# A two-layer encoder on eight cores: pooling sums as one VectorE scan, no tensor work on GpSimd, norms as concurrent tasks

## The chip, the cores and the metric

The kernel runs on all 8 cores of one Trainium2 chip (two dies of four cores). Every core runs the same program on its own tokens; there is no communication between cores. The metric is the device time in microseconds of the slowest core.

## The reference

`x_prompt` is (2, 8192, 1024) and `x_sample` (16, 2048, 1024), both float32. Two layers with their own weights are applied to both. One layer is:

```python
h = rmsnorm(x, g_pre_mix)
u = h @ w_in                      # 1024 -> 6144: pool | B | C | V | gate a | gate b
# pooling: channel group i of 256 has window w = (2, 4, 8, 16)[i]
d = mean(g[t - w/2 .. t + w/2 - 1], valid positions only) - g[t]
y_a = concat(d @ pool_w[i]) * pool_scale
y_b = B * dwconv3_centred(C * V)  # depthwise, over positions
m = sigmoid(ga) * y_a + sigmoid(gb) * y_b
x = x + rmsnorm(m @ w_out, g_post_mix)
f = rmsnorm(x, g_pre_ffn)
hid = silu(f @ w_ffn_gate) * (f @ w_ffn_up)      # 1024 -> 2816
x = x + rmsnorm(hid @ w_ffn_down, g_post_ffn)
```

## The kernel before

Data lie with channels on the 128 partitions and tokens along the free axis. A core has three segments of 2048 tokens (two sample rows, a quarter of a prompt row with a halo), cut into two tiles each: `NT` = 6 tiles a layer and 12 tiles n = 0..11 in all. A tile is some 1032 tokens wide, worked on as two halves i = 0, 1 of w columns. Where the halves of a tile's mixing stage are wider than 512 columns (516 to 528; all tiles but n = 1, 3, 7, 9), `pieces` cuts each half in two, so that a matmul there has 258 to 264 columns and not 512.

The stages of a tile:

- `stage_M` (mixing): 8 channel blocks of 128, three weight units each (`sect` 0 to 2). A unit is a `quad`: a Strassen-Winograd scheme over the two halves with 7 products (P1, P5, P2, P6, P3, P7, P4) of 4 matmuls. It reads seven combinations of h in `h_t`, made beforehand by `combos`, and seven of the weights. Each product is taken out of its PSUM bank by ScalarE (activation, copy to `ss`) or VectorE (`tt` with `ss`, `tm` or `z_t`). `take` and `give` hand out five banks for products and two for copies. Per block, behind the products: `conv` (ScalarE, then two VectorE taps of 1024 columns), `windows` (pooling sums, log2(w) doubling additions of some 1030 columns on GpSimd), and `join` (s1 to s4, four VectorE instructions of 1024 columns).
- `stage_OP`: the output projection, 128 matmuls of 512 columns at most; ScalarE copies to `o_t` and squares for the norm (`Tree`, VectorE adds the squares pairwise).
- `stage_GU`: gate and up as 22 quads; ScalarE does the SiLU, the product with the second half's `up` is made on GpSimd (L982), the first half's on VectorE.
- `stage_D`: down projection, 352 matmuls, also to `o_t`.

The program order of a round n is M(n), 4 units of GU(n-1), OP(n), the other 18 units of GU(n-1), D(n-1). Three background generators run between the PE items: `chain_task` (after OP: post-mix norm, residual with the x tile loaded again, store, pre-FFN norm, `combos`), `post_task` (after D: post-FFN norm, accumulated into DRAM by DMAs of the GpSimd queue) and `pre_task` (x loaded, squared, loaded once more and scaled into `h_t`, `combos`). `rstd` inside them sums over partitions with tiny matmuls (L420), takes the power -0.5 on GpSimd (L434), and sends the row through DRAM (`rsc`) and back to all partitions (`rb`).

Order: the generator keeps a virtual time `stt_["vt"]`, which only `adv` moves, by the matmuls' cost at full clock. `pump` issues what is due: one-shot callbacks (`after`) and steps of the background list `bg`. The list is first in, first out: only its head runs. `finish_bg(tag)` runs everything up to the tagged task to its end at once, without moving the virtual time. Each engine works its instructions strictly in this program order, with semaphore waits derived by `Sched`. VectorE's queue thus holds both PSUM evictions, for which PE waits, and background work.

```python
bg.append([stt_["vt"], gen, tag])                      # L267
tt("pool", zf(Z_T1 + lo, Z_T1 + hi), upr(lo - 1, hi - 1), upr(lo, hi), ALU.add)   # L752
while step * 2 < wd: ...                               # L754, doubling on GpSimd
item(clock["slot"], lambda n=n: finish_bg(("post", n - 2)))                        # L1110
stage_GU(n - 1, 0, 4)
stage_OP(n)
item(..., add_bg(pre_task(n + 1, hold=lambda n=n: gu_done.get(n - 1)), ...))       # L1114
stage_GU(n - 1, 4, JC)
item(clock["slot"], lambda n=n: finish_bg(("chain", n)))                           # L1117
stage_D(n - 1)
```

Weights come as float32 in the first tile of a layer (GpSimd-queue DMAs with a cast), get their Winograd sums on VectorE (`prep`, four additions), and are kept in DRAM; later tiles load them prepared. Four slots hold units in the order of use. Before the first tile, `prologue` folds `pool_w` into the pool columns of `w_in`: 8 groups, both layers, 16 matmuls each.

## Time and profile before

| | us |
|---|---|
| times of 3 runs | 6272.72, 6577.19, 6615.12 |
| median | 6577.19 |
| the profiled execution, its own time | 6255.55 |
| its span on the slowest core (core 1) | 6254.0 |
| spans of the 8 cores | 6207.1 to 6254.0 |
| mean granted TensorE clock, all cores | 0.900 to 0.905 |
| busy: PE, VectorE, ScalarE, GpSimd | 5035.1, 3543.9, 2521.5, 1631.8 |

The span is from the first to the last instruction of one core; the time is the device time of the same execution. The profiled execution lies near the lowest of the three times. Busy PE counts matmuls with modelled ends, so a stage is better judged by matmuls per microsecond. The granted clock is a share of 2.4 GHz; 0.5 is 1.2 GHz.

### The profile page before, as it was taken

How to read it: one execution, taken by the hardware profiler on the slowest of the kernel's cores; microseconds unless marked ns; L12 is line 12 of the kernel's file. 1: busy time of each engine (PE TensorE's matmuls, PEld its weight loads, DVE VectorE, ACT ScalarE, POOL GpSimd, SP SyncE). 2: the span in 40 equal slices, each digit the busy share in tenths (PEclk: the TensorE clock that was granted, in tenths of full speed). 3: DMA queues.
4: the chain of work that ended last, by engine and by line, in shares of the span. 5: the costliest groups of instructions: out<-in, count | busy, mean ns of one | idle time of the engine just before them, and what ended most of it. 6: DMA issues, size and time to landing. Idle time of an engine off the chain costs nothing.

```text
span 6254.0 us, 92792 instructions; the slowest of 8 cores (6207.1 to 6254.0 us)
## 1 busy us (share of the span) xinstructions
PE 5035.1 (81%) x29350; PEld 2934.2 (47%) x29350; DVE 3543.9 (57%) x5521; ACT 2521.5 (40%) x5253; POOL 1631.8 (26%) x1644
## 2 busy tenths in 40 slices
PE   2778875887996897789589897679789789968987
PEld 1543334533433653678467543364334365445433
DVE  3768546554654753754776567275385375465521
ACT  0444433442542452454245353245345244434432
POOL 0323213132231230422323223132143032131221
PEclk6899988998997898899899998889999888979998
DMA  7765885365564464545756559555556454553553
GB/s 168 166 169 139 186 200 136 100 197 133 148 191 117 124 177 132 131 145 171 152 156 203 148 157 222 150 135 163 158 150 189 133 131 138 167 130 113 178 142 91
DMA packets 289209, 959.65 MB, mean 153 GB/s; under 512 B 43098, under 2 KB 44250, under 8 KB 288730
## 3 DMA queue, kind: packets, MB, share of 16 engines
q1 hardware_dynamic: 242074, 838.29, 44.4%
q0 software_dynamic: 46656, 115.43, 12.3%
q8 instruction: 246, 4.03, 0.3%
q14 instruction: 233, 1.91, 0.1%
HBM read 813.27 MB, written 205.32 MB: 163 GB/s over the span
## 4 chain that ended last, share of the span: by engine, by line
PE 57%; DMA 16%; DVE 15%; issue 7%; POOL 2%; ACT 1%; SPq 0%; DVEq 0%; POOLq 0%; ACTq 0%
PE bank L339 57%; DVE z_t L317 4%; DMA x_t<-xss 3%; DMA x_t<-xsin 3%; DMA rb<-rsc 3%; DMA rsc<-r 3%; DVE h_t L317 2%; DVE z_t L308 2%; DVE tm L308 2%; DVE h_t L308 2%; DVE o_t L317 2%; DMA x_t<-xps 1%; DVE slot L308 1%; POOL o_t L308 1%; DMA x_t<-xpin 1%
## 5 line engine op out<-in xcount | busy, mean ns | idle before, releaser
L339 PE MATMUL bank<-h_t,slot 128*128 128x258 f16 (+3 forms) x22064 | 3706.1, 331 | 1049.9 <-DVE tm L308 424.6
L339 PEld LDWEIGHTS bank<-h_t,slot 128*128 128x128 f16 x22064 | 2217.9, 102 | 2503.8 <-issue 1317.5
L339 PE MATMUL bank<-z_t,slot 128*128 128x512 bf16 (+1 forms) x6720 | 1298.4, 356 | 16.2 <-DVE z_t L308 15.3
L303 ACT ACTIVATE ss<-bank 128x258 f32<-128x258 f32 (+3 forms) x1576 | 737.9, 468 | 743.8 <-PE bank L339 732.4
L308 DVE TENSOR_TENSOR sq<-sq 128x512 bf16<-128x512 bf16 (+3 forms) x672 | 366.1, 555 | 1084.2 <-ACT sq L303 1078.5
L339 PEld LDWEIGHTS bank<-z_t,slot 128*128 128x128 bf16 x6720 | 665.1, 99 | 636.8 <-issue 108.0
L303 ACT ACTIVATE bank<-bank 128x512 f32<-128x512 f32 (+3 forms) x788 | 360.3, 457 | 1314.9 <-PE bank L339 1296.1
L308 DVE TENSOR_TENSOR tm<-bank,ss 128x512 f32<-128x512 f32 (+3 forms) x936 | 526.4, 564 | 305.8 <-PE bank L339 240.6
L308 POOL TENSOR_TENSOR z_t<-z_t 128x1038 f32<-128x1038 f32 (+6 forms) x240 | 550.6, 2294 | 534.2 <-ACT z_t L303 494.7
L308 POOL TENSOR_TENSOR z_t<-tm 128x512 bf16<-128x512 f32 (+1 forms) x308 | 376.0, 1221 | 902.2 <-DVE tm L308 550.9
L303 ACT ACTIVATE o_t<-bank 128x512 f32<-128x512 f32 (+1 forms) x448 | 239.2, 534 | 706.6 <-PE bank L339 683.4
L434 POOL TENSOR_TENSOR r<-v,half 128x4 f32<-128x4 f32 (+3 forms) x96 | 107.6, 1121 | 1560.4 <-DVE v L430 1553.5
L303 ACT ACTIVATE sq<-o_t 128x512 bf16<-128x512 f32 (+1 forms) x576 | 362.9, 630 | 311.2 <-POOL o_t L308 267.1
L317 DVE SCALAR_TENSOR_TENSOR z_t<-z_t,cs 128x1024 f32<-128x1024 f32 (+1 forms) x192 | 419.9, 2187 | 27.9 <-ACT z_t L303 14.8
L317 DVE SCALAR_TENSOR_TENSOR o_t<-o_t,cs,rb 128x512 f32<-128x512 f32 (+1 forms) x384 | 375.4, 992 | 101.8 <-DMA rb<-rsc 101.8
L308 DVE TENSOR_TENSOR z_t<-bank,ss 128x258 f32<-128x258 f32 (+3 forms) x640 | 304.9, 476 | 218.1 <-ACT ss L303 113.2
L317 DVE SCALAR_TENSOR_TENSOR z_t<-z_t 128x1024 f32<-128x1024 f32 (+1 forms) x288 | 360.4, 1252 | 7.4 <-POOL z_t L308 3.6
L308 POOL TENSOR_TENSOR o_t<-o_t,x_t 128x512 f32<-128x512 f32 (+1 forms) x192 | 256.4, 1340 | 380.0 <-DVE o_t L317 290.6
L308 DVE TENSOR_TENSOR z_t<-bank,tm 128x512 bf16<-128x512 f32 (+1 forms) x308 | 188.2, 611 | 294.2 <-PE bank L339 293.1
L303 ACT ACTIVATE z_t<-bank 128x258 f32<-128x258 f32 (+3 forms) x640 | 273.0, 426 | 69.0 <-PE bank L339 56.9
L317 DVE SCALAR_TENSOR_TENSOR h_t<-x_t,cs,rb 128x516 f16<-128x516 f32 (+3 forms) x192 | 141.3, 754 | 235.3 <-DMA x_t<-xss 95.4
L308 DVE TENSOR_TENSOR z_t<-tm,z_t 128x258 f32<-128x258 f32 (+3 forms) x320 | 221.7, 693 | 34.7 <-DVE tm L308 1.8
(43 smaller groups left out, 2071.8 us busy)
## 6 DMA issues: line engine op xcount, KB each, us to landing
slot<-wqs SPq DMA_DIRECT2D x460, 896.0 KB, 5.9
wqs<-slot SPq DMA_DIRECT2D x92, 896.0 KB, 6.3
slot<-wds SPq DMA_DIRECT2D x80, 704.0 KB, 4.4
x_t<-xsin SPq DMA_DIRECT2D x128, 256.0 KB, 5.3
x_t<-xss SPq DMA_DIRECT2D x128, 256.0 KB, 5.0
slot<-wgu POOLq DMA_DIRECT2D x44, 512.0 KB, 8.8
slot<-wos SPq DMA_DIRECT2D x40, 512.0 KB, 3.5
rb<-rsc SPq DMA_DIRECT2D x68, 256.0 KB, 6.0
```

What stands on the lines that cost most here:

```text
L303: S.op("act", (lambda a, o=out.ap, i=in_.ap, f=func, kw=kw: a.activation(out=o, in_=i, func=f, **kw)), reads=keys(rd), writes=keys([out]))
L308: v.tensor_tensor(out=o, in0=a, in1=b, op=op)), reads=keys([in0, in1]), writes=keys([out]))
L317: v.scalar_tensor_tensor(out=o, in0=a, scalar=s, in1=b, op0=op0, op1=op1)),
L339: ins = pe.matmul(o, lhsT=a, rhs=b, start=(start and i == 0), stop=(stop and i == n - 1), skip_group_check=True)
L434: S.op("pool", (lambda e, o=r.ap, a=v.ap, b=half[0:bs, 0:nb]: e.tensor_tensor(out=o, in0=a, in1=b, op=ALU.pow)), reads=keys([v]) + [("half ...
```

## The change

- `windows`: for w = 4, 8, 16 the sums over the window are one `tensor_tensor_scan` on VectorE (running sum: add the entering token, subtract the leaving one), and its last value before the tile's end is kept in `hist` for the next tile. For w = 2 it is one subtraction, which replaces s1 as well. The edge correction moves to VectorE.
- The residual addition of the chain and the second half's hidden product go from GpSimd to VectorE. GpSimd keeps small copies and memsets, the power in `rstd`, and its DMAs.
- The two conv taps are issued as two callbacks at different times; the scan is issued after section 2's P7; s1 to s4 are spaced wider.
- `pump` picks the due background task of lowest time, so all tasks run side by side. `finish_bg` now moves the virtual time forward until the tagged task is through. `rstd` of both halves run as tasks of their own; the chain is one task for each half.
- `pre_task(n+1)` no longer waits behind the chain: it squares x during GU(n-1), fills its loads shortly before GU(n-1) ends and scales during D(n-1). The `post` scaling of n-2 is held until M(n) is over and runs in the first 6 units of GU(n-1); OP(n) comes after those 6 units. No `finish_bg` stands ahead of D.
- The first tile's x is loaded once, into `o_t`. Of the weight folds one is made ahead of M(0), three inside it, layer 1's four inside GU(2) and GU(3), each as a unit of the slot ring. OP(0) sits inside M(1)'s first block.
- x buffers 3 to 5, `rb` 2 to 4, `sq` 8 to 7, `ss` 4 to 3. Down-projection matmul groups are issued in parts of 8, with `pump` between them.

```diff
         def pump():
-            while bg and bg[0][0] <= stt_["vt"]:
...
+                t = min(bg, key=lambda q: (q[0], q[1])) if bg else None
+                if t is None or t[0] > stt_["vt"]:
+                    return
+                step(t)
...
-        def finish_bg(tag=None):
-            while bg and (tag is None or any(b[2] == tag for b in bg)):
...
+        def finish_bg(tag):
+            while any(b[3] == tag for b in bg):
+                t = min(bg, key=lambda q: (q[0], q[1]))
+                stt_["vt"] = max(stt_["vt"], t[0])
+                pump()
...
-        def pre_task(n, rate=1.2, hold=None):
+        def pre_task(n, rate=3.5, rate2=3.0, hold=None):
...
+                def side(i=i, tree=tree):
+                    rbs[i] = yield from rstd(tree, w, EPS, pre_mask(l, t, i, w))
+                add_bg(side(), ("prer", n, i))
...
+            order = [(k, i) for kk in range(4) for k in (kk, kk + 4) for i in range(2)]
+            st = Stream([x_src(l, t, k, ha + i * w, ha + i * w + w) for k, i in order], w, 4)
+            if hold is not None:
+                while not hold(8.0):
+                    yield 1.0
+                st.fill()
+                while not hold(0.0):
+                    yield 1.0
...
+        def chain_half(n, i, trees, state):
...
+                stt(o, o, cref(l * C_LAYER + C_POSTMIX + k), rb, ALU.mult, ALU.mult)
+                yield 0.5
+                tt("dve", o, o, x, ALU.add)
...
-                    tt("pool", zf(Z_T1 + lo, Z_T1 + hi), upr(lo - 1, hi - 1), upr(lo, hi), ALU.add)
-                    src, dst, step = Z_T1, Z_T2, 1
-                    while step * 2 < wd:
...
+                    if wd == 2:
+                        tt("dve", dd, upr(ca - 1, cb_ - 1), upr(ca, cb_), ALU.subtract)
...
+                    lo = 17 - h_
+                    out, d0, d1 = zf(Z_T + lo, Z_T + cb_), upr(lo + h_ - 1, cb_ + h_ - 1), upr(lo - 1 - h_, cb_ - 1 - h_)
+                    S.op("dve", (lambda v: v.tensor_tensor_scan(
+                        out=out.ap, data0=d0.ap, data1=d1.ap, initial=hw.ap if second else 0.0,
+                        op0=ALU.add, op1=ALU.subtract)),
+                        reads=keys([d0, d1] + ([hw] if second else [])), writes=keys([out]))
+                    if not second:
+                        copy("pool", hw, zf(Z_T + col(1024) - h_, Z_T + col(1024) - h_ + 1))
...
+                def join():
+                    after(0.3, s3)
+                    after(3.4, s1)
+                    after(4.6, s2)
+                    after(6.0, s4)
...
+                                after(0.8, lambda: tap(0))
+                                after(2.0, lambda: tap(1))
...
-                            tt("pool", hidref(j, w + a0, w + b0), r, s2, ALU.mult)
+                            tt("dve", hidref(j, w + a0, w + b0), r, s2, ALU.mult)
...
+            stage_M(n, (lambda: stage_OP(0)) if n == 1 else None)
+            item(clock["slot"], lambda n=n: finish_bg(("chain", n - 1)))
+            item(clock["slot"], lambda n=n: post_go.add(n - 2))
+            stage_GU(n - 1, 0, PRE)
+            item(clock["slot"], lambda n=n: finish_bg(("post", n - 2)))
+            stage_OP(n)
+            if n + 1 < NN:
+                item(clock["slot"], lambda n=n: add_bg(pre_task(n + 1, hold=pre_hold(n - 1)), ("pre", n + 1)))
+            for j in range(PRE, JC):
+                if n in (3, 4) and j in (12, 16):
+                    add_fold(1, (n - 3) * 2 + (j - 12) // 4)
+                if j == JC - 1:
+                    item(clock["slot"], lambda n=n: gu_near.add(n - 1))
+                stage_GU(n - 1, j, j + 1)
+            stage_D(n - 1)
```

## Rows read from the trace of the kernel before

**Rows 1.** The page: span, busy time of engines, granted clock in 40 slices.
```profile
span 6254.0 us, 92792 instructions; the slowest of 8 cores (6207.1 to 6254.0 us)
...
PE 5035.1 (81%) x29350; PEld 2934.2 (47%) x29350; DVE 3543.9 (57%) x5521; ACT 2521.5 (40%) x5253; POOL 1631.8 (26%) x1644
...
PEclk6899988998997898899899998889999888979998
```

**Rows 2.** Who waited for whom, PE's rows: total us, times, longest us.
```profile
PE bank L339 <- DVE tm L308: 424.6, 136, 17.4
...
PE bank L339 <- DVE h_t L308: 226.0, 11, 30.7
...
PE bank L339 <- DVE h_t L317: 146.9, 9, 18.9
...
PE bank L420 <- DVE sq L308: 77.7, 10, 31.9
```

**Rows 3.** Windows by stage: length, then busy us (and instructions), clock, DMA share, GB/s.
```profile
150.00:398.00 248.00, 176.73 (x1348) 138.95 (x1348) 197.90 (x342) 101.32 (x263) 71.60 (x84) 0.89 0.69 163
...
947.00:984.00 37.00, 1.93 (x12) 1.24 (x10) 13.63 (x22) 1.60 (x3) 1.42 (x2) 0.54 0.59 146
984.00:1225.00 241.00, 192.88 (x1453) 147.72 (x1454) 173.70 (x249) 103.14 (x266) 76.56 (x80) 0.89 0.44 116
1254.00:1383.00 129.00, 113.16 (x519) 48.75 (x517) 85.68 (x121) 61.24 (x110) 48.34 (x37) 0.99 0.74 211
1384.00:1461.00 77.00, 77.00 (x355) 34.73 (x354) 10.33 (x27) 26.19 (x45) 1.05 (x1) 0.98 0.43 134
1498.00:1685.00 187.00, 173.01 (x779) 76.44 (x780) 143.98 (x169) 87.56 (x146) 70.98 (x79) 0.96 0.58 149
1900.00:1940.00 40.00, 40.00 (x154) 16.61 (x153) 4.96 (x13) 12.85 (x22) 0.00 (x0) 0.81 0.33 113
2900.00:2950.00 50.00, 50.00 (x457) 44.58 (x456) 9.75 (x25) 21.46 (x44) 3.42 (x3) 1.00 0.46 134
...
6213.00:6254.00 41.00, 0.42 (x9) 0.28 (x7) 11.44 (x19) 1.23 (x2) 16.28 (x18) 0.54 0.73 115
```

**Rows 4.** Timeline of PE at the start: start us, length, idle before.
```profile
115.68 0.85 PE L420 MATMUL bank<-ones,sq 128*86 128x1 bf16 x6 [20.45 <-DVE sq L308]
...
153.14 7.09 PE L339 MATMUL bank<-h_t,slot 128*128 128x258 f16 x42 [20.39 <-DVE h_t L308]
```

**Rows 5.** Timeline of PE between D(0) and M(2).
```profile
965.40 1.02 PE L339 MATMUL bank<-h_t,slot 128*128 128x258 f16 x4 [17.50 <-DVE h_t L317]
987.77 2.52 PE L339 MATMUL bank<-h_t,slot 128*128 128x258 f16 x11 [21.34 <-DVE h_t L308]
```

**Rows 6.** Timeline inside M(2): one VectorE instruction of 1024 columns, then taps.
```profile
1156.81 1.22 DVE L317 SCALAR_TENSOR_TENSOR z_t<-z_t 128x1024 f32<-128x1024 f32 x1
...
1169.92 1.89 POOL L308 TENSOR_TENSOR z_t<-z_t 128x1024 f32<-128x1024 f32 x1 [2.17 <-ACT z_t L303]
1169.95 4.35 DVE L317 SCALAR_TENSOR_TENSOR z_t<-z_t,cs 128x1024 f32<-128x1024 f32 x2
...
1174.78 5.46 PE L339 MATMUL bank<-h_t,slot 128*128 128x258 f16 x33 [3.21 <-DVE tm L308]
```

**Rows 7.** Groups of instructions by shape: busy us, mean ns, idle before.
```profile
L308 DVE TENSOR_TENSOR tm<-bank,ss 128x512 f32<-128x512 f32 x504 | 344.8, 686 | 175.9 <-PE bank L339 157.0 <-PE bank L420 12.1 <-ACT ss L303 5.8
L317 DVE SCALAR_TENSOR_TENSOR z_t<-z_t,cs 128x1024 f32<-128x1024 f32 x160 | 336.2, 2101 | 26.1 <-ACT z_t L303 14.8 <-DVE z_t L317 5.2 <-POOL z_t L321 0.7
L317 DVE SCALAR_TENSOR_TENSOR o_t<-o_t,cs,rb 128x512 f32<-128x512 f32 x320 | 311.0, 987 | 93.1 <-DMA rb<-rsc 93.1
L308 POOL TENSOR_TENSOR z_t<-tm 128x512 bf16<-128x512 f32 x220 | 303.4, 1379 | 763.9 <-DVE tm L308 488.2 <-ACT tm L303 139.6 <-DVE z_t L317 91.7
...
L308 POOL TENSOR_TENSOR z_t<-z_t 128x1024 f32<-128x1024 f32 x80 | 189.5, 2369 | 152.7 <-ACT z_t L303 143.7 <-POOL z_t L308 0.4
...
L317 DVE SCALAR_TENSOR_TENSOR h_t<-x_t,cs,rb 128x516 f16<-128x516 f32 x80 | 58.6, 754 | 98.4 <-DMA x_t<-xss 48.9 <-DMA x_t<-xsin 40.7 <-DMA x_t<-xps 8.3
```

More of the change, by code:

```diff
@@ L490, in pre_task, with post_task, side @@
+        def post_task(n, trees, hold=None, rate=1.3):
+            l, t = divmod(n, NT)
+            seg, ha, hb, fa, fb = geom(l, t)
+            w = (fb - fa) // 2
+            rbs = [None, None]
+            for i in range(2):
+                def side(i=i):
+                    rbs[i] = yield from rstd(trees[i], w, EPS)
+                add_bg(side(), ("postr", n, i))
             if hold is not None:
@@ L923, in stage_OP, with start @@
             us = [add_plan("o", l, j, first) for j in range(4)]
-            if n == 0:
-                clock["slot"] += 6
-                item(clock["slot"], flush)
-            item(clock["slot"], lambda: add_bg(chain_task(n, trees), ("chain", n)))
+            done = []
+            def start():
+                for i in range(2):
+                    add_bg(chain_half(n, i, trees, done), ("chain", n))
+            item(clock["slot"], start)
             for i in range(2):
@@ L960, in stage_GU @@
             first = t == 0
-            if lo == 0:
-                item(clock["slot"], lambda: finish_bg(("chain", n)))
             for j in range(lo, hi):
```

617 lines of the change are left out of this document (330 added, 287 removed).

## The prediction

> **What bounds the kernel now.** I read the page first, then PE's own waits, then windows cut at the stages' ends, then the timeline in the gaps. On the page [rows 1] TensorE is busy 81% of the span, the others 57% and less. That looks like a PE-bound kernel, but the granted clock swings between 0.6 and 0.9 and the busy time has modelled ends, so I count matmuls. At full clock a matmul of 512 columns costs 77/355 = 0.217 us and one of 258 columns 50/457 = 0.109 us [rows 3]. A tile has 1344 narrow or 672 wide matmuls in M, 128 in OP, 616 in GU, 352 in D: 147 + 28 + 134 + 76 = 385 us, twelve times 4615 us. The span has 1640 us more. Where it goes:
>
> - Between D and the next M. In 947 to 984 PE is busy 1.9 of 37 us [rows 3]. The first matmuls wait 17.5 us for `h_t`, then 21.3 us more for the last of `combos` [rows 5]. In the list of waits these are the `h_t` rows, 226.0 and 146.9 us, and L420 behind the squares, 77.7 us: 451 us [rows 2]. The first tile's part is 20.4 + 15.2 + 52 us (its own two waits and two norm sums, of which the longest, 31.9 us, is in [rows 2], another of 20.45 us in [rows 4]). About 363 us lie at the ten later boundaries. The cause can be read in the code: `pre(n+1)` stands in one list behind `chain(n)`, which ends only as D(n-1) starts.
> - The start. M(0) works from 153 us on [rows 4]; weight folds, norm sums and two passes over x come first, one after the other.
> - M with narrow pieces (8 tiles of 12). 984 to 1225 is M(2) and four GU units: 241 us for 1453 matmuls that cost 147 + 24 = 171 us at full clock, so 70 us are lost. M(3) with 512 columns and the same four units takes 187 against 170 us, 17 lost [rows 3]. The PE row behind it is "DVE tm", 424.6 us in 136 waits [rows 2]: the eviction that frees a bank is late. The timeline shows why. Two conv taps run 4.35 us together beside GpSimd's window additions, and PE waits 3.21 us until an eviction queued behind them is done; a VectorE instruction of the same 1024 columns takes 1.22 us when GpSimd is quiet [rows 6].
> - GU of 18 units with the chain beside it: 129 us against 18 x 28 x 0.217 = 109 us. D runs at its price, 77 us [rows 3].
>
> **Boundaries.** The change lets `pre` square during GU and scale during D. D has VectorE busy 10 of 77 us [rows 3], and `pre` brings 16 scalings of 0.75 us [rows 7] and 16 `combos` (a gap of 0.5 us each is planned), by the planned gaps 16 x 3 + 8 = 56 us of virtual time, less than D's 76. So M starts with D's end. I leave 2 us at each boundary: -343 us. The first matmuls after such a wait run at the 1.2 GHz level (11 in 2.52 us, [rows 5]), some 2.5 us lost each time: -25 us. What would be late next is the last group of `combos`, or the x loads: `Stream` takes from five buffers that two chain halves also use. Bounds: -390 (all gone, clock too) to -190 (half of it stays).
>
> **Start.** x (4.2 MB, once) and the first fold's 1.3 MB at the 163 GB/s of [rows 3] take 34 us; then 5 us for the last squares and sums. From the second norm sum to M's real start it is 37 us now [rows 4], two reloads of x in it. Without them: some 11 us for `rb` through DRAM, then half of the scalings, 11 us, and `combos`, 8 us. M(0) would start at 70 to 75 us: -78, bounds -100 and -40 (a GpSimd queue in which a slot load waits ahead of the power of `rstd`).
>
> **M.** Price of the moved work for each block:
> - Taps: from 2.1 us each [rows 7] to 1.22, apart from each other, so evictions get between them: VectorE -1.8 us, and the 3.2 us stall with the slow clock behind it goes.
> - Scan: no row of before shows one. Nearest rows: 1.22 us for a 1024-column VectorE instruction with two inputs [rows 6], 2.37 us for one GpSimd addition [rows 7]. Each element needs the sum of the one before, so I take the upper, 2.3 us, on 6 blocks of 8; the other two trade s1 for a subtraction at no cost. Beyond the upper end I keep 3 us for the range, since nothing here excludes it.
> - The edge correction and smaller items, 0.2 us.
> - s1 to s4 stay, 1.25 us each, without GpSimd beside them.
>
> The sum of VectorE stays at 17 to 18 us a block against 18.4 us of matmuls, and the longest single hold falls from 4.35 to 2.3 us. I expect a stall of 1 to 2 us at the scan in place of 3 to 5. In addition `post`'s 16 scalings of 0.99 us [rows 7] leave M. Of 70 us lost I keep 30: -40 for each of 7 tiles. M(0) has no `post` beside it and is held by first weights (VectorE 198 of 248 us, [rows 3]), so -10 there. Total -290, bounds -420 and -100. Wide tiles: 17 lost now, -8 each, four tiles, -32; bounds -60 and +20 (the scan costs more than the taps give).
>
> At the scan a rule can be weighed. The row of a plain 1024-column instruction says 1.22 us [rows 6]. The Trainium skill, "DVE: opcode table, instruction layouts, handler registers and perf-mode slots", section Datapath and trigger behaviour, says that the built-in `tensor_tensor_scan` routes its result back to an earlier stage "and runs at half throughput"; by that, an estimate is twice the plain instruction's streaming time, 2.2 to 2.3 us, and with 1.22 us instead the sum would be 6 x 1.1 us x 12 = 79 us of VectorE time lower.
>
> **GU.** The hidden product comes to VectorE, 22 x 0.69 us a tile (the price of a 512-column `tensor_tensor`, [rows 7]), and so do 16 residual additions of 0.69. The 0.99 us of `o_t` scalings should near 0.75 with GpSimd quiet. For the last 16 units: 85.7 us now for 18 units [rows 3], plus 18 x 0.69 + 11 + 8 (`pre`'s squares) - 4, less two units of 2.8 us: 107 us with the old contention counted in, about 95 without it, against 97 us of matmuls. VectorE is then as full as PE. The evictions hide their own latency with five banks; I take 7.0 us a unit, as now (7.2), 112 us. The first six units carry `post`: 16 scalings, 12 us of VectorE in 36 us, +3. The sum for ten tiles is -20, bounds +250 and -150. GU(11) has `post` drained ahead of it at present; spread out, -12. GU(0) and GU(6) stay with their first weights' DMAs. The removed GpSimd product costs PE nothing: it was off the path.
>
> **Folds** move from the start, where they were the cover of nothing, into M(0), GU(2), GU(3): 1.3 MB each, 8 us at 163 GB/s if DMA is what is short, seven times: between 0 and +60, I take +20. The tail [rows 3] stays at 41 us: scalings and stores after the last D have no cover, before or after.
>
> **Sum.** -368 - 78 - 290 - 32 - 20 - 12 + 20 = -780. From the profiled execution's 6255.6 us (its span is 6254.0) this gives 5476, rounded 5470 us, 12.5% less. The median shown, 6577, lies 5% above that profiled execution, the lowest of the three times at it. So a median of the new kernel can lie 5% above my sum, 5745, without any step being wrong; this sets the upper end as much as the rivals do.
>
> **Rivals.**
> 1. VectorE becomes the bound in GU. For: 95 to 107 us of it in 97. Against: D and the first units have room, and the last 16 units can run late into D only by program order, which holds evictions back too. Price: 8.5 in place of 7.0 us a unit, 24 us a tile in 11 tiles: +265, 5735 us.
> 2. The boundary stays half. For: two chain halves and `pre` share five x buffers and one `lock` for the norm's bank, so `pre` can miss GU's end. Against: 97 us of GU for 56 us of planned steps and 20 of `rstd`. Price: 18 us x 10: 5650 us.
> 3. TensorE's granted clock. In 1900 to 1940 it is 0.81 while PE works without a gap, and 154 matmuls take 40 us; in other D stages it is 1.00 [rows 3]. If the filled stretches everywhere got 0.81, OP and D alone, 104 us a tile, would cost 24 us more each, M and GU (281 us a tile) half their share of 66: 290 + 400 us, some 6150. Against: most gapless stretches of before have the full clock. The Trainium skill, "TensorE: Matmul & The Clock Gate", section Part 1: The HAM clock gate, tells of a current limiter that takes a die to 13/16 when three of its cores run dense matmuls; by that rule the gain would shrink to this rival's, and the trace bears it out only in a few stretches.
> 4. Slower than before. VectorE works in order, and now in all of GU its queue holds instructions that wait for x loads of three streams and for `rb`: some 50 a tile, 600 in all, each with evictions behind it. Place: GU, and D. It decides from 1.7 us of wait for each: 600 x 1.7 = 1020 us eats the gain and takes the time to 6490 us. For: in the gaps of before, scalings do wait for x. Against: the new code waits 7 us of virtual time after each load before it issues the user, and the loads land in that time.
>
> **Chances.** Forecast 0.66, rival 1 0.12, rival 2 0.10, rival 3 0.08, rival 4 0.04. The range takes in rivals 1 and 2 and the 5% between profile and median: 5250 (boundaries and M at their good ends) to 5750. Faster by over 2% (about what a measurement of this kernel can tell from no change): all but rival 4 and a bit of the unknown, 0.94; within 2% 0.02; slower 0.04.
>
> **What would show it.** Right: no gap over 5 us between D and M; `h_t` waits of PE under 60 us in all; M(0) working by 75 us; M(2) with its GU part at 1344 matmuls in 175 us; scan rows near 2.3 us, tap rows near 1.2; GpSimd below 500 us busy; VectorE about 3600 us, now two thirds of the span. Wrong: `o_t` or `tm` waits growing in GU (rival 1), L420 waits of PE in GU (a norm sum in PE's queue ahead of its squares), clock at 0.81 in long stretches (rival 3), or DMA-landing waits on VectorE in GU (rival 4).

## The result, and the profile after

The changed kernel's median over 4 runs is 5723.02 us (5587.19 to 5843.98), the kernel before's in the same comparison 6424.95 (6201.3 to 6615.12). The ratio is 0.899, with a 95% interval of 0.873 to 0.925: 10% faster, as 5626.05 / 6255.55 = 0.899 of the two profiled executions says too. On the median that was shown of before, 6577.19, this ratio gives 5912 us, above the end of my range; the forecast 5476 / 6255.6 is a ratio of 0.875. The direction and the places were right, the size was 150 us too good in the profiled execution (5626 against 5476). Some executions have a die at a lower clock than the other; they are left out of the ratios here and below.

The page of the changed kernel: span, busy time of the engines, granted clock in 40 slices, and the DMA issues of the x tiles (times issued, KB, median us to landing).

```profile
span 5624.5 us, 92366 instructions; the slowest of 8 cores (5556.1 to 5624.5 us)
...
PE 4900.8 (87%) x29350; PEld 2861.8 (51%) x29350; DVE 3453.4 (61%) x6113; ACT 2517.9 (45%) x5253; POOL 417.4 (7%) x844
...
PEclk9899899999999989999997998999999999999998
...
x_t<-xsin SPq DMA_DIRECT2D x128, 256.0 KB, 8.5
```

Against [rows 1], GpSimd has lost 1214 us of busy time and VectorE has not gained any, although the product, the additions and the scans are now its own: 3453 in place of 3544 us. PE's clock no longer falls to 0.6 or 0.7 slice after slice. The groups by shape say why VectorE stayed level: mean ns of one is the second number behind the bar.

```profile
L332 DVE SCALAR_TENSOR_TENSOR z_t<-z_t,cs 128x1024 f32<-128x1024 f32 x160 | 205.0, 1282 | 69.8 <-ACT z_t L318 64.9 <-DVE z_t L332 4.9
L332 DVE SCALAR_TENSOR_TENSOR o_t<-o_t,cs,rb 128x512 f32<-128x512 f32 x320 | 234.8, 745 | 13.5 <-DMA rb<-rsc 13.5
L323 DVE TENSOR_TENSOR z_t<-tm 128x512 bf16<-128x512 f32 x220 | 151.1, 687 | 21.4 <-ACT tm L318 10.8 <-DVE tm L323 9.2 <-DVE v L468 0.5
```

The groups by line give the scans, in both forms (the second has a constant as its initial value):

```profile
L893 DVE TENSOR_TENSOR_SCAN z_t<-z_t,hist 128x1031 f32<-128x1031 f32 (+5 forms) x36 | 84.8, 2355 | 0.0
L893 DVE TENSOR_TENSOR_SCAN z_t<-z_t 128x1031 f32<-128x1031 f32 (+8 forms) x36 | 82.8, 2300 | 0.1
```

A tap fell from 2101 to 1282 ns and an `o_t` scaling from 987 to 745 once GpSimd was quiet [rows 7]; the hidden product is 687 ns on VectorE against 1379 on GpSimd. That gives back 131 + 76 us. Other groups fell too, for instance the pairwise sums of squares (`sq`, 128x512) from 574 to 423 ns, another 71 us. All of it together pays for the 168 us of scans, the products and 133 us of residual additions.

PE's waits by what ended them (total us, times, longest us), largest first, with ScalarE's own waits for the squares:

```profile
ACT sq L318 <- DVE o_t L323: 200.9, 134, 8.9
...
PE bank L354 <- ACT bank L318: 174.0, 77, 9.5
PE bank L354 <- DVE z_t L323: 143.1, 124, 5.7
...
PE bank L354 <- ACT ss L318: 124.4, 82, 11.8
ACT sq L318 <- DMA x_t<-xss: 114.8, 40, 9.8
...
PE bank L354 <- DVE tm L323: 112.1, 128, 10.0
ACT sq L318 <- DMA x_t<-xsin: 90.3, 27, 9.0
...
PE bank L459 <- DVE sq L323: 37.6, 2, 23.9
```

The 451 us of boundary waits in [rows 2] are gone (what is left of `h_t` and of the sums is the first tile's, below), and `tm` fell from 424.6 to 112.1. New at the top are waits of PE for ScalarE, 174.0 + 124.4 us, where before had 80.4 + 65.9. ScalarE itself waited for the x loads and for the residual additions before it could square.

The timeline of PE at the start, to be held against [rows 4]:

```profile
41.61 0.85 PE L459 MATMUL bank<-ones,sq 128*86 128x1 bf16 x6 [23.90 <-DVE sq L323]
...
69.50 1.02 PE L354 MATMUL bank<-h_t,slot 128*128 128x258 f16 x4 [12.50 <-DVE h_t L332]
81.37 2.74 PE L354 MATMUL bank<-h_t,slot 128*128 128x258 f16 x12 [10.85 <-DVE h_t L323]
```

Windows by stage on core 3 (columns as in [rows 3]). In order: M(0); M(2) with six GU units; the other 16 units of GU(1); D(1); M(3) with six units; the tail.

```profile
70.00:322.00 252.00, 188.28 (x1447) 145.07 (x1445) 204.77 (x406) 106.21 (x273) 24.60 (x69) 0.93 0.74 182
844.00:1052.00 208.00, 188.27 (x1512) 144.22 (x1511) 155.41 (x261) 110.06 (x279) 21.38 (x55) 1.00 0.54 144
1082.00:1222.00 140.00, 106.59 (x469) 45.05 (x467) 88.00 (x161) 63.62 (x114) 5.54 (x5) 0.93 0.86 215
1222.00:1298.00 76.00, 76.00 (x353) 34.42 (x352) 23.78 (x47) 18.41 (x30) 0.31 (x2) 1.00 0.37 126
1298.00:1481.00 183.00, 180.31 (x841) 81.49 (x840) 147.44 (x179) 94.98 (x159) 20.28 (x48) 1.00 0.60 163
5575.00:5624.00 49.00, 0.84 (x11) 0.50 (x8) 11.44 (x19) 1.23 (x2) 16.09 (x18) 0.54 0.73 97
```

D(1) ends at 1298 and M(3) begins there: the gap of 37 us [rows 3] is zero. M(2) with six units takes 208 us for some 1510 matmuls, where 241 us stood for 1453. M(3) with its six runs at PE's price. But GU's last 16 units take 140 us for 469 matmuls, where 18 units took 129: 8.8 us a unit in place of 7.2. (Over the eight cores it is 134 to 142 us.) The places of gain and of loss are thus in plain sight, and the third line is the one that I had not forecast. VectorE is busy 88.00 of 140 us in it, ScalarE 63.62, and the 16 DMA engines 0.86 of it. Waits in this window alone (total us, times, longest us):

```profile
ACT sq L318 <- DMA x_t<-xsin: 29.3, 10, 8.6
PE bank L354 <- ACT bank L318: 15.7, 4, 8.4
...
PE bank L354 <- ACT ss L318: 10.1, 4, 5.1
...
PE bank L354 <- DVE tm L323: 7.5, 4, 2.5
```

What one of the stalls in that window looks like, in the timeline of all engines:

```profile
1113.38 0.69 DVE L323 TENSOR_TENSOR o_t<-o_t,x_t 128x512 f32<-128x512 f32 x1 [3.17 <-DMA x_t<-xsin]
...
1114.16 0.63 ACT L318 ACTIVATE sq<-o_t 128x512 bf16<-128x512 f32 x1 [4.29 <-DVE o_t L323]
...
1117.50 0.58 ACT L318 ACTIVATE bank<-bank 128x512 f32<-128x512 f32 x1
1118.22 9.45 PE L354 MATMUL bank<-h_t,slot 128*128 128x512 f16 x36 [5.56 <-ACT bank L318]
```

An x load lands late; the residual addition waits 3.17 us for it at the head of VectorE's queue; the square waits 4.29 us at the head of ScalarE's; two more squares and then a copy from bank to bank, which PE needs to accumulate onto, stand behind; PE waits 5.56 us. The load's median time to landing is 8.5 us on the page and 10.1 us in this window, and the planned order allows 7 us (`XLAT`).

### The profile page after: what moved, and what is told of

Same layout as the page of the kernel before. It is cut to its first block, busy times and chain, and to the rows that moved or that the text cites. A ratio compares the mean times of both kernels' runs of the same rounds, so it can differ in the third digit from the quotient of the medians.

```text
span 5624.5 us, 92366 instructions; the slowest of 8 cores (5556.1 to 5624.5 us)
## 1 busy us (share of the span) xinstructions
PE 4900.8 (87%) x29350; PEld 2861.8 (51%) x29350; DVE 3453.4 (61%) x6113; ACT 2517.9 (45%) x5253; POOL 417.4 (7%) x844
## 4 chain that ended last, share of the span: by engine, by line
PE 63%; DMA 18%; DVE 10%; issue 5%; ACT 2%; SPq 1%; DVEq 0%; POOL 0%; ACTq 0%; POOLq 0%
PE bank L354 62%; DMA rsc<-r 4%; DMA x_t<-xsin 3%; DMA x_t<-xss 3%; DVE z_t L323 3%; DVE z_t L332 2%; DMA x_t<-xps 2%; DMA rb<-rsc 2%; DVE tm L323 2%; SPq L346 1%; DMA x_t<-xpin 1%; DVE o_t L332 1%; DVE z_t L893 1%; DMA slot<-wqs 1%; DMA slot<-wgu 1%
## 5 line engine op out<-in xcount | busy, mean ns | idle before, releaser
L354 PE MATMUL bank<-h_t,slot 128*128 128x258 f16 (+3 forms) x22064 | 3613.4, 323 | 609.1 <-ACT bank L318 174.0
L323 DVE TENSOR_TENSOR sq<-sq 128x512 bf16<-128x512 bf16 (+3 forms) x672 | 281.9, 423 | 867.9 <-ACT sq L318 866.6
L332 DVE SCALAR_TENSOR_TENSOR z_t<-z_t,cs 128x1024 f32<-128x1024 f32 (+1 forms) x192 | 246.3, 1283 | 86.2 <-ACT z_t L318 81.2
L332 DVE SCALAR_TENSOR_TENSOR o_t<-o_t,cs,rb 128x512 f32<-128x512 f32 (+1 forms) x384 | 282.5, 745 | 13.5 <-DMA rb<-rsc 13.5
L318 ACT ACTIVATE sq<-x_t 128x512 bf16<-128x512 f32 (+3 forms) x176 | 110.9, 630 | 310.2 <-DMA x_t<-xss 114.8
L472 POOL TENSOR_TENSOR r<-v,half 128x4 f32<-128x4 f32 (+1 forms) x96 | 113.0, 1177 | 1773.3 <-DVE v L468 1773.2
L318 ACT ACTIVATE tm<-tm 128x512 f32<-128x512 f32 (+1 forms) x308 | 173.2, 562 | 119.1 <-DVE tm L323 113.5
L323 DVE TENSOR_TENSOR o_t<-o_t,x_t 128x512 f32<-128x512 f32 (+1 forms) x192 | 132.6, 690 | 135.8 <-DMA x_t<-xss 51.3
L323 DVE TENSOR_TENSOR z_t<-tm 128x512 bf16<-128x512 f32 (+1 forms) x308 | 188.0, 610 | 23.0 <-ACT tm L318 11.5
L323 DVE TENSOR_TENSOR slot<-slot 128x512 f16<-128x512 f16 x368 | 147.7, 422 | 85.6 <-DMA slot<-wgu 28.9
```

What stands on the lines that cost most here:

```text
L318: S.op("act", (lambda a, o=out.ap, i=in_.ap, f=func, kw=kw: a.activation(out=o, in_=i, func=f, **kw)), reads=keys(rd), writes=keys([out]))
L323: v.tensor_tensor(out=o, in0=a, in1=b, op=op)), reads=keys([in0, in1]), writes=keys([out]))
L332: v.scalar_tensor_tensor(out=o, in0=a, scalar=s, in1=b, op0=op0, op1=op1)),
L354: ins = pe.matmul(o, lhsT=a, rhs=b, start=(start and i == 0), stop=(stop and i == n - 1), skip_group_check=True)
L472: S.op("pool", (lambda e, o=r.ap, a=v.ap, b=half[0:bs, 0:nb]: e.tensor_tensor(out=o, in0=a, in1=b, op=ALU.pow)), reads=keys([v]) + [("half ...
```

## The experiments

My theory for GU (theory A): `pre`'s first pass beside the chain puts loads that land late at the head of in-order queues, ScalarE's above all. The rival from the prediction is VectorE's load. A third candidate, theory C below, is DMA bandwidth. The notation "M+6" is a narrow M with its six GU units, "GU-16" the other 16 units of a tile with 512-column pieces and without weight folds. The changed kernel has M+6 at 208 us and GU-16 at 140 us in round n = 2 and 144 in n = 8, both on its slowest core (129 to 144 in n = 8 over all cores). Where a text below names no other round, GU-16 is that of n = 2.

**e1_pre_in_mix, e2_lat9, e3_pass1_no_load, e4_scan_twice** ran on one chip. The first starts `pre(n+1)` with M(n), not after OP(n); the second also allows x loads 9 us.

```diff
-XLAT = 7.0
+XLAT = 9.0                                   # e2 alone
@@ at the start of M(n)
+                    add_bg(pre_task(n + 1, hold=pre_hold(n - 1)), ("pre", n + 1))
@@ behind stage_OP(n)
-                item(clock["slot"], lambda n=n: add_bg(pre_task(n + 1, hold=pre_hold(n - 1)), ("pre", n + 1)))
```

> The changed kernel with one thing moved: the first pass of pre(n+1) (16 loads of x, 16 squares on ScalarE, the norm sums) is started at the start of M(n) and not after OP(n), so GU holds only the chain. Theory A (in GU, ScalarE and VectorE stand in program order behind x loads that land later than the 7 us of virtual time left for them, and PSUM copies for PE wait behind): the last 16 GU units of a middle tile fall from some 140 us to 115 to 120 us, M grows by at most 5 us, in all 150 to 230 us off the changed kernel's profiled 5624.5 us. Theory B (VectorE is full in GU, rival 1 of the prediction): pre's squares are 6 of some 88 us of VectorE there, so GU falls by under 6 us a tile and the time by under 60 us. Theory C (DMA bandwidth in GU is short whatever the order): between the two, with GU about 125 us.

> The kernel of e1 with 9 us instead of 7 us of virtual time between an x load and the instruction that uses it. Theory A: the waits of VectorE and ScalarE for x_t in GU shrink further and GU ends 3 to 8 us earlier a tile than in e1 (another 30 to 80 us in all), less some 10 us by which M(1) starts later. Theory B or C: no change against e1, or a few us worse.

The third keeps the instructions in place, but the first pass squares a resident buffer. So it leaves out 16 loads of x a tile, its norms come from other data, and four x buffers are left for the chain.

```diff
-                    r = yield from st.get()
+                    r = (yield from st.get()) if hold is None else tref(x_t, "x", NX - 1, 0, w)
```

> The changed kernel where the first pass of pre for tiles 2 to 11 squares one resident x buffer and loads nothing (so the pre-mix norms of these tiles come from other data); the squares, adds and norm sums stay in GU as they were, and four x buffers are left for the chain. Theory A: like e1, GU's last 16 units at 115 to 125 us, since the work stays and only the waits for loads go. If the squares' own ScalarE time (16 x 0.63 us) or their place in its queue were the cause, GU stays at 135 to 145 us.

The fourth issues every scan twice.

> The changed kernel with each scan issued twice (same output): 72 more VectorE instructions of 2.3 us, 166 us in all, in M. If M has VectorE time to spare and only the length of one hold counts, narrow tiles grow by at most 8 us and the time by 30 to 90 us; if M is VectorE-bound after the change, nearly all 166 us and more show up, as 12 to 25 us a tile.

Their profiled executions took 5617.96, 5502.29, 5562.56 and 5839.93 us, the changed kernel's 5626.05. Windows: M(2) with six units, then the last 16 units of GU(1). First e1 (core 6):

```profile
837.00:1054.00 217.00, 191.84 (x1521) 145.81 (x1519) 160.97 (x277) 117.39 (x295) 23.54 (x57) 0.98 0.60 159
1083.00:1205.00 122.00, 104.95 (x465) 45.26 (x464) 83.84 (x145) 56.22 (x99) 3.39 (x3) 0.94 0.76 208
```

e2 (core 7):

```profile
840.00:1056.00 216.00, 191.06 (x1524) 145.50 (x1522) 160.79 (x277) 117.99 (x295) 23.42 (x57) 0.99 0.62 159
1085.00:1197.00 112.00, 99.68 (x465) 43.54 (x463) 83.63 (x146) 55.77 (x99) 3.70 (x3) 1.00 0.86 225
```

e3 (core 6):

```profile
1086.00:1212.00 126.00, 104.55 (x470) 44.70 (x469) 87.75 (x162) 63.67 (x115) 7.68 (x5) 0.96 0.80 206
```

e4 (core 5):

```profile
880.00:1107.00 227.00, 196.35 (x1513) 149.37 (x1512) 170.29 (x267) 109.81 (x279) 21.36 (x55) 0.95 0.51 132
```

e1 shortens GU-16 by some 20 us, as theory A had it, but lengthens M+6 by 9, where the loads, squares and their sums now lie; over the whole run nothing is left of the 150 to 230 us that I expected. e2 brings GU-16 to 112 us, the very length I had forecast, with VectorE as busy in it as before (83.63 against 88.00 us). So 84 us of VectorE fit into 112, and its load was not what made GU long. e3 is the weakest of the three: with the same instructions in the same order, and only the first pass's loads taken away, GU-16 falls to 126. On the slowest cores the last 16 units of rounds 2 to 11 (first weights and folds included) add up to 1395 us in the changed kernel, 1324 in e3, 1271 in e1 and 1212 in e2: taking away the first pass's loads gives 71 of e2's 183 us, four tenths. The rest goes when its squares leave and the chain's own loads get their time. Within these stretches PE waited behind ScalarE 217 us in the changed kernel, 112 in e3, 113 in e1 and 64 in e2, and behind VectorE 59, 118, 99 and 77. So what ScalarE holds up is the largest part of the change, but it does not by itself order e1 and e3. (In whole runs `bank` plus `ss` are 298.4, 181.6, 265.9 and 150.8 us; e1's squares cause such waits in M.)

Not all of the 183 us are waits. The matmuls of these stretches were busy 1111 us in the changed kernel and 1046 in e2, at a mean granted clock of 0.91 and 0.96. In the changed kernel, from 1162 to 1182 us, behind 10 us in which PE was busy only 4.0, the granted clock averages 0.66 and 0.70 in two slices of 10 us, so part of that time is at the 1.2 GHz level. Some 65 of the 183 us are thus slower matmuls, 17 of them in GU(5), where the clock was 0.82.

Theory C, DMA bandwidth, is not ruled out for a part. Length times GB/s gives 30.1 MB in the changed kernel's GU-16, 25.9 in e3, 25.4 in e1 and 25.2 in e2; length times DMA share gives 120, 101, 93 and 96 us of all 16 engines. The forecast 112 us would have had to move 30.1 MB at 269 GB/s. These windows reach 225 at most, and the fastest GU stretch of the changed kernel (round 9 on core 4, 118 us) 253; at these rates 30.1 MB take 134 and 119 us, an estimate. On the other hand e1 and e2 move the same bytes, and e2, with 9 us allowed to a load, is 10 us shorter: time allowed counts beside bytes. The median landing of an x load in these windows follows the DMA share: 5.0 us at 0.74 in the kernel before, 8.1 at 0.76 in e1, 9.0 at 0.80 in e3, 10.1 in the changed kernel and 10.8 in e2, both at 0.86. No run changed the bytes alone, so the two can't be parted fully.

e4 answers for M: 6 x 2.33 = 14 us of scan more in a tile lengthen M+6 by 19 us, and the whole run by 214 us, where 168 us of instructions were added. M pays for VectorE time in full and more, although VectorE is busy only 155 of 208 us: the scan holds up evictions that PE waits for, in spite of VectorE's idle time elsewhere. The two scans stand back to back, though, so e4 raises the sum and also makes one hold of 4.7 us out of 2.3; it does not tell the two apart. The mean granted clock of the stretch is 0.95 in place of 1.00.

**e5_hid_add_gpsimd** puts the hidden product and the residual addition back on GpSimd.

```diff
-                tt("dve", o, o, x, ALU.add)
+                tt("pool", o, o, x, ALU.add)
-                            tt("dve", hidref(j, w + a0, w + b0), r, s2, ALU.mult)
+                            tt("pool", hidref(j, w + a0, w + b0), r, s2, ALU.mult)
```

> The changed kernel with two operations back on GpSimd as before: the second half's hidden product and the chain's residual addition. VectorE loses 500 instructions of 0.69 us, 340 us. If VectorE's load held GU (rival 1 of the prediction), GU's last 16 units fall by 10 us or more a tile. If it is issue order and landing times, GU stays at 130 to 145 us or grows by up to 10 us, since o_t scalings go from 0.75 towards 0.99 us beside GpSimd and ScalarE's squares wait for an addition of 1.3 us in place of 0.7.

The profiled execution took 5762.36 us; its cores 0 to 3 have spans of 5606.0 to 5654.9. The same GU-16 as above, on core 0:

```profile
1094.00:1243.00 149.00, 114.35 (x474) 46.97 (x473) 76.61 (x131) 63.57 (x115) 46.44 (x37) 0.89 0.85 203
```

VectorE has 11 us less to do than in the changed kernel and GU-16 is 9 us longer; on cores 0 to 3 it is 136 to 150 us, on the changed kernel's 134 to 142. So it did not get shorter. The moved operations are slower on GpSimd (1.38 and 1.34 us), so this run alone could hide a small relief. With e3, which gets 126 us out of the same 88 us of VectorE, rival 1 of the prediction falls: VectorE's load did not bound GU.

**e6_before_scan** is the kernel before with the window sums (and their edge correction) on VectorE, nothing else.

```diff
-                    tt("pool", zf(Z_T1 + lo, Z_T1 + hi), upr(lo - 1, hi - 1), upr(lo, hi), ALU.add)
...
+                        S.op("dve", (lambda v: v.tensor_tensor_scan(
+                            out=out.ap, data0=d0.ap, data1=d1.ap, initial=hw.ap if second else 0.0,
+                            op0=ALU.add, op1=ALU.subtract)), ...)
```

> The kernel before with one part of the change: the window sums (w = 4, 8, 16 as the scan, w = 2 as one addition) and the edge correction on VectorE, at the place and time where they stood on GpSimd; tasks, start and the paired taps as before. My reading of M (GpSimd beside the taps doubled them, 4.35 us a pair): tap rows fall from 2.1 to about 1.25 us; the scan takes 2.3 us; narrow tiles gain 5 to 15 us of the 40 that the whole change gave, and the time falls by 50 to 120 us with all ten boundary gaps in place. If VectorE's sum is what counts, nothing or a loss of up to 60 us, since scan and contention cancel.

It took 6238.02 us (the kernel before 6422.23 on that chip and 6255.55 in its profiled execution on another, too far apart to read the expected 50 to 120 us from). A tap takes 1287 ns in it, where before has 2101: with nothing but the window sums and the edge correction gone from GpSimd, the taps are as short as in the changed kernel. Its M(2) with four units, on core 3:

```profile
968.00:1218.00 250.00, 193.75 (x1457) 148.09 (x1458) 170.10 (x282) 103.65 (x267) 35.48 (x58) 0.87 0.46 124
```

From the first matmul, at 965.40 [rows 5], to the end of the four units, at 1225 [rows 3], before took 260 us, the boundary's second wait among them; here it is 250. The scan in place of the GpSimd additions, by itself, gives 10 us of the 33 and more that M(2) gained. The rest of M's gain came with other edits (`post`'s scalings gone from M, s1 to s4 spaced wider, `h_t` ready at once), which I did not separate, except for the taps by the next run.

**e7_taps_together** issues both taps in one callback.

```diff
-                                after(0.8, lambda: tap(0))
-                                after(2.0, lambda: tap(1))
+                                after(0.8, lambda: (tap(0), tap(1)))
```

> The changed kernel with both conv taps issued in one callback, one behind the other (2.5 us hold) and not 1.2 us of virtual time apart. If the length of a single VectorE hold sets the stalls in M (my reading of the tap pair before), narrow tiles grow by 5 to 10 us each, 40 to 80 us in all. If it is the sum of VectorE's work, no change (under 15 us).

5679.44 us profiled; M+6 on core 0:

```profile
858.00:1067.00 209.00, 189.39 (x1512) 144.41 (x1513) 157.31 (x262) 108.94 (x277) 29.00 (x55) 1.00 0.52 145
```

209 us in place of 208. Issuing the taps apart is thus worth 1 us a tile. The prediction had argued from the longest single hold of VectorE; that is not decided here, since the pair takes 2.68 us and the scans of 2.3 us are there in both kernels.

**e8_defer_squares** adds to e2 that the chain's squares and stores come one step later, so that a square never follows at once on the addition that waits for a load. It also brings the chain to its end ahead of D (`finish_bg`).

```diff
-                tree.push(o)
-                dma("sp", x_dst(l, t, k, a, a + w), o, ("xst", i * KC + k))
+                if k > 0:
+                    tree.push(oref(i, k - 1, 0, w))
+                    dma("sp", x_dst(l, t, k - 1, a, a + w), oref(i, k - 1, 0, w), ("xst", i * KC + k - 1))
...
@@ ahead of stage_D(n - 1)
+            item(clock["slot"], lambda n=n: finish_bg(("chain", n)))
```

> The kernel of e2 with the chain's square of o(k) and its store issued one step later, behind the residual addition of k+1, as the kernel before had it. Theory A, extended (every instruction that is issued too soon on ScalarE holds the PSUM copies behind it; in e2 ScalarE's squares still waited 290 us for VectorE's residual additions): these waits fall under 120 us and GU ends 3 to 8 us earlier a tile, 30 to 80 us in all against e2. If these waits are only ScalarE's spare time, nothing changes (within 20 us of e2's profiled 5502).

5562.48 us on another chip than e2's 5502.29, its cores from 5426.4 to 5560.9; the 30 to 80 us that I expected are not there. Waits on core 0 of e8, two rows:

```profile
PE bank L354 <- DVE tm L323: 204.5, 146, 12.9
...
PE bank L354 <- ACT bank L318: 37.0, 33, 5.1
```

The waits behind ScalarE are gone as meant (37.0 us where e2 has 111.5), but those behind VectorE's `tm` have grown (e2: 147.8), and GU-16 is 112 to 116 us on the eight cores, as in e2 (110 to 118). In the GU stretches of rounds 2 to 11, PE waited behind ScalarE 7 us (core 0) where e2 has 64 (core 7), and behind VectorE 119 where e2 has 77. Most of the wait changed its name. ScalarE was therefore where the stall showed, and not all of its cause; the late load holds up VectorE's queue too.

**e9_pre_at_D, e10_best, e11_folds_spread, after_again** shared one chip. e9 is the test from the other side: the changed kernel, with `pre(n+1)` let in only when the chain is through.

```diff
@@ behind stage_OP(n)
-                item(clock["slot"], lambda n=n: add_bg(pre_task(n + 1, hold=pre_hold(n - 1)), ("pre", n + 1)))
@@ ahead of stage_D(n - 1)
+            item(clock["slot"], lambda n=n: finish_bg(("chain", n)))
...
+                item(clock["slot"], lambda n=n: add_bg(pre_task(n + 1, hold=pre_hold(n - 1)), ("pre", n + 1)))
```

> The changed kernel with one part undone in effect: pre(n+1) is added only after chain(n) is through, as D(n-1) starts, as the kernel before had it. If the ten boundary gaps went because pre no longer waits behind the chain, they come back, 36 us or more each (pre's planned steps are 132 us against 76 of D): 360 to 700 us in all, less 100 to 200 us since GU is as free of pre's loads as in e1 (115 to 125 us). If something else closed them (the deeper x stream, the side tasks of the norm), the gaps stay under 10 us each and the time falls as GU does.

It took 6162.28 us, where the changed kernel's second profile on this chip took 5731.1. PE's timeline on core 6 after D:

```profile
827.79 5.56 PE L354 MATMUL bank<-z_t,slot 128*128 128x512 bf16 x25
...
841.82 0.85 PE L459 MATMUL bank<-ones,sq 128*86 128x1 bf16 x6 [5.41 <-DVE sq L323]
861.60 0.85 PE L459 MATMUL bank<-ones,sq 128*86 128x1 bf16 x6 [18.93 <-DVE sq L323]
887.25 1.02 PE L354 MATMUL bank<-h_t,slot 128*128 128x258 f16 x4 [24.80 <-DVE h_t L332]
```

and its GU-16, behind M+6 of 214 us:

```profile
1129.00:1246.00 117.00, 111.16 (x477) 47.50 (x476) 85.39 (x148) 57.65 (x101) 3.39 (x3) 0.91 0.76 214
```

The gap after D is back, 54 us here and 50 to 63 us at ten boundaries, 538 us in all. GU-16 itself, from its first matmul to its last, takes 114 us, and 112 to 118 on the eight cores, where the changed kernel on the same chip has 131 to 141. This one run shows both sides: `pre` beside the chain is what fills the boundaries, and it is also what costs GU some 22 us.

e10 is e8 with 12 us for `pre`'s loads and 8.5 for the others, the norm's row `rb` used 1.5 us later, closer steps at the end of the chain (0.9 for a scaling, 0.5 for `combos`), and the four folds of layer 1 spread over rounds 2 to 5, one in each. e11 is the changed kernel with that spreading alone:

```diff
-                if n in (3, 4) and j in (12, 16):
-                    add_fold(1, (n - 3) * 2 + (j - 12) // 4)
+                if n in (2, 3, 4, 5) and j == 14:
+                    add_fold(1, n - 2)
```

> The changed kernel itself on this chip, as the measure for the next ones: GU's last 16 units 130 to 148 us in middle tiles, narrow M with six GU units 208 us.

> What the runs so far point to, put together: e8 (first pass of pre in M, users of loads 8.5 us and in M 12 us behind the load, squares one step later), rb used 1.5 us later, and layer 1's four folds one a round in GU(1) to GU(4) and not two in each of GU(2) and GU(3). Theory A: GU at 105 to 112 us without a fold and 115 to 120 with one, M with six units 208 to 214, and 2 to 4% less time than the changed kernel on the same chip. If order no longer matters, it equals the changed kernel within 1%.

> The changed kernel with layer 1's four folds one a round in four rounds and not two in each of two. In e2 the GU stages with two folds took 130 to 137 us and those without 110. If a fold costs a fixed 10 us, the sum stays as it is: two rounds get shorter by 10 us, two longer. If the cost is the ring of four slots running dry behind two folds close together, 10 to 20 us are saved in all.

The changed kernel took 5731.1 us, e10 5583.94 (2.6% less), e11 6040.66. e11's whole time can't be read for folds. Its clock was 0.849 to 0.875 on all cores. Two of its D stages on core 0:

```profile
800.00:894.00 94.00, 94.00 (x362) 39.26 (x361) 23.80 (x47) 18.83 (x31) 2.75 (x6) 0.81 0.69 180
4718.00:4795.00 77.00, 77.00 (x362) 35.24 (x360) 23.68 (x47) 18.86 (x31) 0.11 (x1) 1.00 0.37 125
```

The same 362 matmuls without a gap take 94 us at 0.81 and 77 at 1.00. On cores 4 and 5, where D in rounds 2 to 5 took 76 to 79 us, the four GU stretches with the folds add up to 578 and 583 us, in the changed kernel on the same chip to 558 and 572: spreading gave nothing there. In the order of e8 and e10 it was not isolated; e8's two rounds with two folds each have GU-16 at 129 to 139 us, e10's four rounds with one fold at 116 to 122 on core 2, its rounds 8 to 10 without one at 109 or 110.

**e12_best_again and e13_after_same_chip** are e10's kernel and the changed kernel once more, on one chip.

> The same kernel as e10, timed in five rounds on a chip that it shares with the changed kernel, since on the last chip the granted clock stood at 0.81 for 640 to 1630 us of each core in both. Theory A: the stages repeat (GU 108 to 118 us, M with six units 208 to 215), and the time is 2 to 3% under the changed kernel's. If most of the gain is given back through a lower granted clock (PE is busier), the stages at full clock still shrink but the time comes out within 1%.

> The changed kernel beside e12 on the same chip: GU 128 to 148 us in middle tiles, M with six units 208 us; the measure for e12.

To before, e12 has 0.871 [0.862, 0.879] and e13, the changed kernel, 0.894 [0.885, 0.903]. The intervals lie apart; the best version is 0.871 / 0.894 = 0.974 of the changed kernel, and its profiled execution, 5485.62 us, is within 10 us of my forecast's 5476. Windows of e12 on core 3:

```profile
848.00:1060.00 212.00, 189.01 (x1522) 144.62 (x1521) 160.97 (x277) 118.33 (x295) 25.62 (x57) 1.00 0.63 162
1090.00:1211.00 121.00, 105.24 (x477) 45.84 (x475) 85.68 (x152) 55.16 (x98) 4.59 (x5) 0.96 0.87 221
```

and of e13 on core 5:

```profile
839.00:1049.00 210.00, 190.26 (x1521) 145.10 (x1519) 151.98 (x262) 106.03 (x272) 18.47 (x53) 1.00 0.49 140
1095.00:1234.00 139.00, 108.51 (x468) 45.60 (x467) 87.58 (x161) 63.66 (x114) 5.54 (x5) 0.90 0.87 216
```

M+6 is as long in both; the difference is in GU-16, 121 against 139 us, though a fold lies in it in e12 and none in e13.

## Why the prediction was right and where it failed

- **What bounds, and the boundaries.** Right. The part of PE's waits that I put down to the ten boundaries, 363 us, is gone, and e9 brings the gaps back by moving `pre` alone. Forecast -343 and -25 for the clock. I can't part those two in the trace; together they were forecast at -368, and the waits alone are 363. Rival 2 (half a boundary) did not happen.
- **Start.** Right: the full stream of M(0) starts at 81.4 us in place of 153.1, -72 against -78. The forecast had it working by 75; its first four matmuls ran at 69.5.
- **Scan and taps.** 2.30 and 2.36 us for a scan against 2.3 taken, 1.28 us for a tap against 1.22. The Trainium skill ("DVE: opcode table, instruction layouts, handler registers and perf-mode slots", section Datapath and trigger behaviour) says that the built-in scan runs at half throughput. The trace agrees: 2.30 us is 1.9 times the plain instruction's 1.22.
- **Narrow M.** Right in size; the reason is open. M+6 is 208 us where its 1512 matmuls cost 183.5: 25 us lost, I had kept 30. The wide tiles without first weights lose nothing (183 us) where I had kept 9. I had argued from "the longest single hold falls from 4.35 to 2.3 us". e4 makes the longest hold 4.7 us again and costs 19 us a tile, but it adds 13.8 us to VectorE's sum as well; e7 makes a hold of 2.68 us for 1 us a tile. Hold and sum are not told apart.
- **GU: the step that failed.** "The evictions hide their own latency with five banks; I take 7.0 us a unit, as now (7.2), 112 us". Measured on core 3: 126 to 144 us in six of the rounds without folds or first weights, 7.9 to 9.0 a unit, and 111 in the last, the only one of these rounds in which no `pre` runs beside GU. Over the rounds n = 2 to 11 the last 16 units add up to 1395 us on core 3, where ten times 112 and some 45 for GU(6)'s first weights (the trace of before has 170 us there, other rounds about 126) make 1165: 230 us over. Some 60 came back elsewhere, in M and the first six units, better than forecast, and in D, 772 us over these rounds where before had 813 (mean granted clock 0.99 and 0.95), which I had left unchanged. All rounds n = 2 to 11 gained 513 us, forecast 681. I had counted VectorE's microseconds (95 to 107 forecast, 88 found), no waits at the heads of the queues, and no DMA time for the 16 loads (4.2 MB) that `pre` brings into a stretch where the DMA engines were 0.74 busy already [rows 3]. `pre`'s squares stand in the same in-order queue of ScalarE as the PSUM copies, and the chain's additions in VectorE's, behind loads that take 8.5 us where 7 is allowed. e2 removes `pre`'s first pass, allows the chain's loads 9 us and gets 112; e9 removes `pre` and gets 114; e3 removes only the loads and gets 126; e5 takes load off VectorE and gets nothing; e8 keeps ScalarE clear of the waits and gets no more than e2, so it is not ScalarE alone. Of the loss itself, some two thirds are waits of PE and one third slower matmuls behind them.
- **Rival 1** has nearly the measured number, 8.5 us a unit and 24 us a tile, by luck: its reason, a full VectorE, is refuted by e2 and e3 (84 us of it in 112, 88 in 126).
- **Rival 4** had this mechanism mainly in the wrong engine and at the wrong price: 600 waits of 1.7 us on VectorE. The trace has 105 waits of ScalarE's squares for x loads, 310 us, not all of which reach PE, and 50 of VectorE's residual additions, 121 us. I had given it a chance of 0.04. Its argument against, that "the new code waits 7 us of virtual time after each load ... and the loads land in that time", is what did not hold; in before's trace it looks true (a median landing of 5.3 us), and I had asked nothing about landing under the new traffic, 215 GB/s in GU-16 with three streams of x.
- **Folds** were forecast at +20 in all. In the changed kernel the two rounds with two folds each stand 4 and 8 us over round 2; in e2, where GU is short, 25 and 18 us (136.9 and 129.3 against 111.5). I read this so, without a run for it: a fold fills slack that other waits leave, and once they are gone it costs its own time.
- **Smaller terms.** GU(11) -18 (forecast -12), the tail +8 (forecast 0). GpSimd 417 us busy (below 500), VectorE 3453 (about 3600 forecast, since I had `o_t` scalings and taps at more).
- **Rival 3 (clock).** Nearly absent in the changed kernel's profile: D(1) is at 1.00, but on cores 2, 3, 6 and 7 the clock was 0.81 for some 150 us. On core 3 that took in the end of GU(5) and most of D(5), which lasted 85.6 us where D(4), as many matmuls, took 77.6. And after_again, e10 and e11 on another chip had 0.81 for longer parts of the run, in e11 for the first six D stages of core 0 (93 us each, 76 in the other six). The price I gave it, some 17 us for each D, is what e11 shows (94 against 77). By the rule in the Trainium skill, "TensorE: Matmul & The Clock Gate", section Part 1: The HAM clock gate, all of these kernels' gapless stages would be limited to 13/16. Most are not (the D stages of e12 take 76 to 78 us, at 1.00), so the measurement decides against it as a general rule here, and for it as a risk.
- **From the sum to the median.** I gave the sum, made against 6255.6, as the predicted time, and took the 5% between the profiled execution and the median only into the range. A ratio carries over, a difference does not: even 0.875 of 6577 is 5757, already past my upper end. With the mended GU, 0.899 of it is 5912. The failed term and this step together put the result outside.

What stays open: how the 28 us of GU-16 divide between the instructions in ScalarE's and VectorE's queues, the lateness of loads and the DMA time of the bytes themselves (e3, which takes away both the waiting for the first pass's loads and their bytes, gets half of it in round 2 and four tenths over the ten rounds); and what of M's gain is due to which of its edits.

## What to carry to other kernels

When background work is moved under a stage, count each in-order queue that it enters, not only the busiest engine: a square that waits for a load holds the PSUM copy behind it, and PE with it. Add the bytes that it brings to those of the stage, and see what rate the forecast length would need (269 GB/s here, where the fastest GU stretch of the changed kernel reached 253). Compare the time allowed for a load with its landing time under the new traffic, and allow more where it lands late (from 7 to 9 us took the run from 5618 to 5502 us). Boundaries and start gave 435 of the 630 us gained; when forecasting, carry the ratio and not the difference to a median from another execution.

## What the runs showed of the hardware

- GpSimd's window additions beside them made VectorE's 1024-column taps 1.6 times as long: 2101 ns on average, 1287 in e6, where only these additions (and the edge correction) left GpSimd, 1282 in the changed kernel. The 512-column scaling takes 987 ns before, 941 in e6, 820 in e5 and 745 in the changed kernel. Taking work from GpSimd to VectorE left VectorE's total lower than before (3453 against 3544 us).
- An x load of 256 KB lands in 5.0 us (median) where the DMA engines are 0.74 busy and in 10.1 us where they are 0.86 busy.
- A scan whose initial value is read from SBUF takes 2355 ns, with a constant 2300.
- One execution (e11, core 0) had TensorE at 0.81 through six dense D stages, others at 1.00, with the same instructions; D's length follows the clock, 94 against 77 us.
